# A hybrid decoder layer: weights scaled on ScalarE, slopes folded into the queries, the value tile in quarters

## The reference, cut to what matters

```python
def index_scores(qi, wi, ki, qpos, kpos):
    s = jnp.einsum('bthd,bsd->bths', qi, ki).astype(jnp.float32) * (IDX_DIM ** -0.5)
    s = jnp.einsum('bths,bth->bts', jax.nn.relu(s), wi.astype(jnp.float32))
def sparse_attend(q, k_sel, v_sel, qpos, sel):           # mixer A
    logits = jnp.einsum('bthd,btkhd->bhtk', q, k_sel).astype(jnp.float32) * (HEAD_DIM ** -0.5)
    dist = (qpos[None, :, None] - sel).astype(jnp.float32)
    logits = logits - alibi_slopes()[None, :, None, None] * dist[:, None]
    p = jax.nn.softmax(logits, axis=-1).astype(v_sel.dtype)
    return jnp.einsum('bhtk,btkhd->bthd', p, v_sel)
def forget_attend(q, k, v, Fq, Fk, qpos, kpos):          # mixer B
    logits = jnp.einsum('bthd,bshd->bhts', q, k).astype(jnp.float32) * (HEAD_DIM ** -0.5)
    logits = logits + (Fq.T[:, :, None] - Fk.T[:, None, :])
    p = jax.nn.softmax(logits, axis=-1).astype(v.dtype)
    return jnp.einsum('bhts,bshd->bthd', p, v)
```

## Time and profile before

| | us |
|---|---|
| median of three runs | 1120.89 |
| the profiled execution | 1125.59 |
| its span, first to last instruction | 1123.4 |
| TensorE busy | 1005.9 (90%) |
| VectorE busy | 571.9 (51%) |
| ScalarE busy | 399.5 (36%) |
| GpSimd busy | 170.0 (15%) |
| head pairs 1 to 8 | 125.5 to 418.0 |

### The profile page before, as it was taken

The page is one execution under the profiler, slowest core; times in us unless marked ns, Lnnn a source line. Parts: engine busy times, 40 slices in busy tenths (PEclk is TensorE's granted clock), DMA queues, the critical chain, the costliest instruction groups (busy, mean ns, idle before and its releaser), DMA issues.

```text
span 1123.4 us, 20111 instructions
## 1 busy us (share of the span) xinstructions
PE 1005.9 (90%) x7616; PEld 917.1 (82%) x7616; DVE 571.9 (51%) x1299; ACT 399.5 (36%) x803; POOL 170.0 (15%) x122
## 2 busy tenths in 40 slices
PE   8798878998899889549989999599989999998998
PEld 6596666887788778547389999489989999998998
DVE  3544799776575661554038844564433224443232
ACT  3344444444445442112064544443421113332111
POOL 3003222322342232230003232000000000000000
PEclk9899989998999899778979999799999999999999
DMA  9431521322121224783616665323222333332322
GB/s 351 135 82 33 158 76 48 87 57 57 47 76 48 59 57 120 231 270 121 235 57 206 189 205 176 89 57 94 85 75 87 91 93 94 93 91 71 90 66 76
DMA packets 184106, 124.54 MB, mean 111 GB/s; under 512 B 14419, under 2 KB 168083, under 8 KB 184036
## 3 DMA queue, kind: packets, MB, share of 16 engines
q1 hardware_dynamic: 183906, 123.50, 36.5%
q10 hardware_dynamic: 130, 0.10, 0.0%
HBM read 116.99 MB, written 6.59 MB: 110 GB/s over the span
## 4 chain that ended last, share of the span: by engine, by line
PE 79%; DVE 8%; DMA 4%; ACT 3%; issue 3%; POOL 2%; SPq 1%; ACTq 0%; DVEq 0%; POOLq 0%
PE bank L863 21%; PE bank L864 20%; PE bank L865 20%; DMA qbc<-q_d 3%; PE bank L968 2%; PE bank L945 2%; PE bank L954 2%; PE bank L1116 1%; POOL prod L770 1%; PE bank L782 1%; PE bank L1007 1%; PE bank L804 1%; PE bank L986 1%; DVE w_lo L1725 1%; PE bank L923 1%
## 5 line engine op out<-in xcount | busy, mean ns | idle before, releaser
L863 PE MATMUL bank<-h_hi,w_hi 128*128 128x260 f32 x1360 | 411.0, 302 | 32.9 <-DVE h_lo L1668 17.7
L864 PE MATMUL bank<-h_lo,w_hi 128*128 128x260 f32 x1360 | 400.1, 294 | 0.0
L865 PE MATMUL bank<-h_hi,w_lo 128*128 128x260 f32 x1360 | 399.1, 293 | 0.0
L863 PEld LDWEIGHTS bank<-h_hi,w_hi 128*128 128x128 f32 x1360 | 273.2, 201 | 50.0 <-issue 41.7
L864 PEld LDWEIGHTS bank<-h_lo,w_hi 128*128 128x128 f32 x1360 | 273.3, 201 | 0.2
L865 PEld LDWEIGHTS bank<-h_hi,w_lo 128*128 128x128 f32 x1360 | 272.6, 200 | 0.0
L740 POOL TENSOR_TENSOR w_lo<-raw,w_hi 128x1024 fp32r<-128x1024 f32 x44 | 104.8, 2381 | 420.5 <-ACT w_hi L1311 253.7
L863 PE MATMUL bank<-u_hi,w_hi 128*128 128x260 f32 x512 | 146.5, 286 | 7.7 <-DVE u_lo L2120 7.7
L2105 DVE TENSOR_TENSOR w_lo<-raw,w_hi 128x1024 fp32r<-128x1024 f32 x62 | 76.0, 1226 | 145.7 <-ACT w_hi L1543 145.7
L864 PE MATMUL bank<-u_lo,w_hi 128*128 128x260 f32 x512 | 146.0, 285 | 0.0
L865 PE MATMUL bank<-u_hi,w_lo 128*128 128x260 f32 x512 | 145.9, 285 | 0.0
(11 more groups left out here) (317 smaller groups left out, 1320.3 us busy)
## 6 DMA issues: line engine op xcount, KB each, us to landing
raw<-in_w_in SPq DMA_DIRECT2D x44, 512.0 KB, 3.7
raw<-in_w_ada SPq DMA_DIRECT2D x32, 512.0 KB, 4.0
raw<-in_w_up SPq DMA_DIRECT2D x32, 512.0 KB, 3.9
raw<-in_w_down SPq DMA_DIRECT2D x32, 512.0 KB, 3.9
ada<-in_w_ada SPq DMA_DIRECT2D x4, 2048.0 KB, 12.7
kv<-in_cache_k_b SPq DMA_DIRECT2D x16, 256.0 KB, 3.0
qbc<-q_d SPq DMA_DIRECT2D x16, 256.0 KB, 4.4
kv<-in_cache_k_a SPq DMA_DIRECT2D x16, 256.0 KB, 3.4
```

What stands on the lines that cost most here:

```text
L863: mm(out, hi[:, k, :], x_h, start=first and k == ks[0], stop=False)
L864: mm(out, hi[:, k, :], x_l, start=False, stop=False)
L865: end = mm(out, lo[:, k, :], x_h, start=False, stop=last and k == ks[-1])
```

## The change

Five edits. `probs` on VectorE becomes a reciprocal alone, and the scaling an activation on ScalarE, at the head of its slot. The slope of mixer A isn't multiplied into the distances any more: the queries are divided by it (gq gets five columns), and exp multiplies by it. The value tile's halves are projected in quarters of 12 matmuls, in slots 4, 5, 6 and 7. The low halves of weights are made on VectorE in pair 0 and from pair 4 on, and on GpSimd in pairs 1 to 3. The index scores go through banks 4 to 7 instead of 4 and 5.

```diff
-HALVES_AT = [0, 1, 2, 3, 4, 6]
+HALVES_AT = [0, 1, 2, 3, 5, 7]
+FIRST_HALF_AT = [4, 6]
+        gq = new("gq", [P, 5])
+        def unit_slope(U):
+            m, c = pair_mixer(U // 8)
+            return SLOPES[2 * c + U % 2] if m else 1.0
@@ GpSimd
+            link(pool.memset(gq_scale[:, 0:1], QK_SCALE))
+            for hh in range(2):
+                for c in range(H // 2):
+                    last = pool.memset(gq_scale[64 * hh:64 * hh + 64, 1 + c:2 + c], QK_SCALE / SLOPES[2 * c + hh])
...
             for p, s in ITERATIONS:
-                for i in split_at(p, s):
-                    rest_w(i)
+                if 1 <= p <= 3:
+                    for i in split_at(p, s):
+                        rest_w(i)
@@ TensorE
+            def project(i, half, ks=range(NCH)):
+                if ks[0] == 0:
...
+                end = half_tile(i, half, bank[half + 4 * par(i)][:, 0:HALF], ks, first=ks[0] == 0, last=ks[-1] == NCH - 1)
+                if ks[-1] == NCH - 1:
+                    end.then_inc(proj_done, 1)
             def index_scores(n):
-                if n >= 2:
-                    pe.wait_ge(idx_relu, n)
+                if n >= 4:
+                    pe.wait_ge(idx_relu, n - 2)
...
-                    mm(bank[4 + hh][:, 0:width(qb)], q_idx[rows, h // 2, qb * P:(qb + 1) * P], ki2[rows, 0:width(qb)],
+                    mm(bank[4 + n % 4 + hh][:, 0:width(qb)], q_idx[rows, h // 2, qb * P:(qb + 1) * P], ki2[rows, 0:width(qb)],
@@ TensorE, in the iterations
-                if s in HALVES_AT and (p, s) < (N_PAIRS + 1, 4):
+                if s < 4:
                     project(T_PAIR + 3 * p + HALVES_AT.index(s) // 2, HALVES_AT.index(s) % 2)
+                elif p <= N_PAIRS:
+                    if s in FIRST_HALF_AT:
+                        project(T_PAIR + 3 * p + 2, FIRST_HALF_AT.index(s), range(4))
+                    else:
+                        project(T_PAIR + 3 * p + 2, HALVES_AT.index(s) % 2, range(4, NCH))
@@ ScalarE
-                A(lg[:, U % 3, 0:w], lg[:, U % 3, 0:w], ACT.Exp, bias=stat[:, 8 + U % 8:9 + U % 8],
+                A(lg[:, U % 3, 0:w], lg[:, U % 3, 0:w], ACT.Exp, bias=stat[:, 8 + U % 8:9 + U % 8], scale=unit_slope(U),
...
+            def probs(U):
+                w = width(U % 8 // 2)
+                act.wait_ge(inv_ready, U + 1)
+                A(lg[:, U % 3, 0:w], lg[:, U % 3, 0:w], ACT.Copy, scale=stat[:, 26 + U % 2:27 + U % 2]).then_inc(p_ready, 1)
...
                 before = slot_before(p, s)
+                if 0 <= U - 1 < N_UNITS:
+                    probs(U - 1)
@@ VectorE
-                    if U == 32:
-                        dve.wait_ge(stored, 64)
...
-                    link(dve.tensor_scalar(abias[:, 0:w], src, SLOPES[2 * c + hh], None, ALU.mult))
                     dve.wait_ge(s_done, U + 1)
-                    link(dve.tensor_tensor_reduce(out[:, 0:w], s_bank[:, 0:w], abias[:, 0:w], 1.0, TAKEN, ALU.add, ALU.max, mx))
+                    link(dve.tensor_tensor_reduce(out[:, 0:w], s_bank[:, 0:w], src, 1.0, TAKEN, ALU.add, ALU.max, mx))
...
-            def probs(U):
-                w = width(U % 8 // 2)
+            def inverse_sum(U):
                 dve.wait_ge(e_ready, U + 1)
-                link(dve.reciprocal(stat[:, 25:26], stat[:, 16 + U % 8:17 + U % 8]))
-                dve.tensor_scalar(lg[:, U % 3, 0:w], lg[:, U % 3, 0:w], stat[:, 25:26], None, ALU.mult).then_inc(p_ready, 1)
+                dve.reciprocal(stat[:, 26 + U % 2:27 + U % 2], stat[:, 16 + U % 8:17 + U % 8]).then_inc(inv_ready, 1)
@@ VectorE, in the iterations
                 if p == 0:
+                    for i in split_at(p, s):
+                        rest_w(i)
...
+                if p >= 4:                     # after logits(U)
+                    for i in split_at(p, s):
+                        dve.wait_ge(lo_ready, i)
+                        rest_w(i)
```

More of the change, by code:

```diff
@@ L173, in layer @@
         g_col = new("g_col", [P, 2])
-        gq = new("gq", [P, 2])
+        gq = new("gq", [P, 5])
         gk_row = new("gk_row", [P, 2, HD])
@@ L219, in layer @@
         p_t = new("p_t", [P, 2, 2, QB, P])
+        gq_scale = sb("gq_scale", [P, 5], F32, place["at"])[0]
         place["at"] += 8192
@@ L373, in layer @@
         e_ready = sem("e_ready")
+        inv_ready = sem("inv_ready")
         p_ready = sem("p_ready")
@@ L403, in layer @@
         s_consts = sem("s_consts")
+        gq_consts = sem("gq_consts")
         kip_landed = sem("kip_landed")
@@ L728, in _ @@
             pool.memset(s8[:, 11, :], 0.0).then_inc(s_consts, 1)
+            link(pool.memset(gq_scale[:, 0:1], QK_SCALE))
+            for hh in range(2):
+                for c in range(H // 2):
+                    last = pool.memset(gq_scale[64 * hh:64 * hh + 64, 1 + c:2 + c], QK_SCALE / SLOPES[2 * c + hh])
+                if hh == 0:
+                    link(last)
+            last.then_inc(gq_consts, 1)
             def power(n):
@@ L892, in first_tiles @@
                                 last.then_inc(proj_done, 1)
[L894 to L903, removed]
+            def project(i, half, ks=range(NCH)):
+                if ks[0] == 0:
+                    if half == 0:
+                        pe.wait_ge(hi_ready, i + 1)
+                        pe.wait_ge(lo_ready, i + 1)
+                    if i >= 1:
+                        before = i - 1 if par(i - 1) == par(i) else i - 2
+                        pe.wait_ge(act_evac, act_evac_value(before, half))
+                end = half_tile(i, half, bank[half + 4 * par(i)][:, 0:HALF], ks, first=ks[0] == 0, last=ks[-1] == NCH - 1)
+                if ks[-1] == NCH - 1:
+                    end.then_inc(proj_done, 1)
             def ada_product(g, half):
@@ L1374, in store_back @@
             def store_back(p, kd):
-                m = pair_mixer(p)[0]
+                m, c = pair_mixer(p)
+                col = 1 + c if m else 0
                 act.wait_ge(back_done, 2 * p + kd + 1)
@@ L1379, in store_back @@
                         act.wait_ge(s_done, 8 * (p - 1))
-                    A(q_fm[:, p % 2, :], bank[3][:, :], ACT.Copy, scale=gq[:, m:m + 1]).then_inc(back_read, 1)
+                    A(q_fm[:, p % 2, :], bank[3][:, :], ACT.Copy, scale=gq[:, col:col + 1]).then_inc(back_read, 1)
                 else:
@@ L1401, in relu_scores @@
                     act.wait_ge(smt_done, 1)
-                A(rbuf[:, n % 2, 0:w], bank[4 + n % 2][:, 0:w], ACT.Relu).then_inc(idx_relu, 1)
+                A(rbuf[:, n % 2, 0:w], bank[4 + n % 4][:, 0:w], ACT.Relu).then_inc(idx_relu, 1)
             def ada_rows(g):
@@ L1745, in _ @@
             dve.wait_ge(small_landed, 16 * N_SMALL)
-            dve.tensor_scalar(gq[:, :], g_col[:, :], QK_SCALE, None, ALU.mult)
+            dve.wait_ge(gq_consts, 1)
+            dve.tensor_tensor(gq[:, 0:1], gq_scale[:, 0:1], g_col[:, 0:1], ALU.mult)
+            dve.tensor_tensor(gq[:, 1:5], gq_scale[:, 1:5], g_col[:, 1:2].to_broadcast([P, 4]), ALU.mult)
             def index_sum(n):
@@ L1807, in logits @@
                                                   ALU.add, ALU.max, mx))
-                dve.tensor_scalar(nm, mx, -1.0, None, ALU.mult).then_inc(lg_ready, 1)
-            def probs(U):
-                w = width(U % 8 // 2)
+                dve.tensor_scalar(nm, mx, -unit_slope(U), None, ALU.mult).then_inc(lg_ready, 1)
+            def inverse_sum(U):
                 dve.wait_ge(e_ready, U + 1)
-                link(dve.reciprocal(stat[:, 25:26], stat[:, 16 + U % 8:17 + U % 8]))
-                dve.tensor_scalar(lg[:, U % 3, 0:w], lg[:, U % 3, 0:w], stat[:, 25:26], None, ALU.mult).then_inc(p_ready, 1)
+                dve.reciprocal(stat[:, 26 + U % 2:27 + U % 2], stat[:, 16 + U % 8:17 + U % 8]).then_inc(inv_ready, 1)
             def mean_squares(p, kd):
@@ L1949, in _ @@
                 if 0 <= U - 1 < N_UNITS:
-                    probs(U - 1)
+                    inverse_sum(U - 1)
                 if 0 <= U < N_UNITS:
                     logits(U)
+                if p >= 4:
+                    for i in split_at(p, s):
+                        dve.wait_ge(lo_ready, i)
+                        rest_w(i)
                 if p < N_PAIRS:
```

## The result

The changed kernel took 1112.13 us (median of 11 runs, 1105.13 to 1115.97) against 1121.73 for the kernel before (median of 11, 1118.17 to 1125.46): a ratio of 0.991, 95% interval 0.9885 to 0.9935. The direction was right. The size was not: 9.6 us against a forecast of 32, and 1112 lies outside the range of 1068 to 1107. The profiled execution lasted 1115.97 us, its span 1114.0 against 1123.4.

A forecast was written before the change was run, and what follows sets the result against it. The attention stage was taken as a four-engine loop whose latency shows twice a pair, where the clock can fall too. Pair gains plus 1.2 at the end sum to 32 us: 1125.6 to 1093.6 profiled, median 1089; range 1068 to 1107.

The forecast's parts named there:

- the sum of pairs 1 to 3: Pairs 0 and 1 together -10 us, pair 2 -3.1, pair 3 -2.6, though the scale waits behind VectorE's reciprocal.
- Pair 0: Four index-score banks remove 9.5 us of waits; late forget rows leave 2.3 there; with pair 1, -10 us (bounds 5 and 14).
- Pair 3: VectorE and the keys' chain set the pace; 35.2 us taken for pairs 2 and 3 alike, so -2.6 here.
- Pairs 4 to 7: Quarters shorten slots 4 to 7: 34.3, then 33.4 us each, including 0.7 for a slow stretch behind the keys' wait.
- The scale's price: 64 more ScalarE activations at 0.35 to 0.65 us, 4.0 us a pair, duration hidden.
- The slopes: Folding the slopes removes a VectorE operation that ran while waiting for scores: gain 0 (bounds 0 and 2 us).
- The last low half: End of the attention stage, before the store of queries: 1.23 us on VectorE replaces 2.43 on GpSimd, -1.2.
- B: Rival: ScalarE's queue blocks, half a us lost in each of slots 4 to 7, 16 us in all: 1105; chance 0.14.
- D: Rival: slower, two more engine crossings cost 1.0 us a unit, 64 us uncovered: 1153; chance 0.06.
- A: Rival: keys' chain doesn't bind, clock stays at 2.4 GHz; -50 us, 1071; chance 0.15.
- C: Rival: the port; VectorE's low halves meet GpSimd's power, ten times 1.6 us from pair 4 to 8: 1105; chance 0.04.
- E: Rival: all hidden anyway, pairs stay and pair 0's gain is lost; within 5 us, 1119; chance 0.06.

The follow-up runs named there:

- recip_early: Changed kernel, but in pairs 1 to 4 VectorE takes the reciprocal in the middle of the selection round; 1098.41 us, ratio 0.9806.
- only_scale: Kernel before with one edit: the scaling as an activation at the head of ScalarE's slot; 1134.89 us, ratio 1.0111.
- only_scale_ordered: Kernel before with scaling on ScalarE, but page copies ahead of the scale and the reciprocal in the middle of the selection round; 1119.65 us, ratio 0.9978.
- low_on_gpsimd: Changed kernel, but the low halves stay on GpSimd from pair 4 on too; 1107.04 us, ratio 0.9878.
- fbc_first: Changed kernel, but SP loads the forget rows of pair 1 before the 48 page transfers; 1103.53 us, ratio 0.9846.
- all_orders: Changed kernel: page copies before scale, reciprocal mid selection round, forget rows before pages, low half behind mean and last o_lo from pair 4; 1090.48 us.
- orders_low_five: all_orders with slot 4's low half moved behind the keys' multiplications, to the end of slot 5; 1084.40 us, ratio 0.966.
- scale_late: Changed kernel, but VectorE scales in pairs 1 to 3 (units 0 to 23) as before; 1113.39 us, ratio 0.9925.
- orders_scale_late: orders_low_five, but VectorE scales in pairs 1 to 3, its reciprocal after the selection round; 1100.30 us, ratio 0.9816.
- only_quarters: Kernel before with one edit: the value tile projected in quarters; 1110.56 us, ratio 0.9887.

## Why the prediction was wrong, step by step

*The step that failed* is the sum of pairs 1 to 3. The prediction wrote that the scale waits "behind VectorE's reciprocal, which stands behind the selection round", and priced it: "the squares of slot 4 and GpSimd's w_lo are later by about 1.2 us". It named the right wait, and followed it to two of the instructions behind it. It left out the page copies and z_s, which stand there too and hold banks that TensorE wants: 3.0, 4.3 and 3.0 us in single waits, where the prediction had 1.2 us in slot 4. It also took the result to be "needed two slots later": that counts from the scores; from the scale it is one slot, and it didn't bind (no wait at L973 is over 1.2 us). Forecast for pairs 0 and 1 together -10, measured -1.5; pair 2 -3.1, measured +4.8; pair 3 -2.6, measured +2.0. That is 21.0 of the 22.4 us by which the profiled execution missed the sum. The bounds did not hold it either: "0 and the 6.5 us" for pairs 2 and 3 had no loss in them, though a new wait at the head of a queue can cost, and that was the second error. The cause is shown by recip_early (-13.7 us with the work unchanged, the waits for ki_pt 0.5 for 7.4) and by only_scale against only_scale_ordered (15 us). The parts done alone don't add up to the whole: quarters -12.5, banks -4.4, scale +11.9, and +5.1 for the low halves from pair 4 on (the changed kernel less low_on_gpsimd) give 0.1; measured -9.6. Which parts help each other is not shown, and pair 0's low halves and the slopes had no run of their own.

*Pair 0* went as argued as far as fbc. Rows of the tile after, 100 to 130 us, beside the earlier trace rows:

```profile
L591 SPq DMA_DIRECT2D fbc<-negf_d x4: 433/594/1672, 115.7 to 124.1; - x4
L1977 DVE TENSOR_TENSOR fdiag<-fbc,cmask x2: 691/692/693, 121.6 to 122.4; 128x512 f32<-128x512 f32 x2
...
  DMA fbc<-negf_d: 5.5, 1
```

VectorE waited 5.5 us and started at 121.6, where 121.7 was forecast. The slot 2 wait of TensorE came as well (3.0 us), but through ScalarE: z_s behind the scale behind VectorE. That VectorE would then need only 31 us for the pair did not come true: it took 39.1, to 160.7. fbc_first shows what the late forget rows cost: 8.6 us.

*Pair 3* was given pair 2's 35.2 us without a look at its own row: TensorE was busy for 35.5 us there, 2.4 more than in pair 2; among other things a step of the sample group stands in its slot 6 (32 matmuls of 8 columns, L1029 before, 3.74 us). The 35.5 us are no floor, for part of them ran at 1.2 GHz. all_orders shows pair 3 at the full clock:

```profile
184.76:222.26 37.50, 33.18 (x274) 28.82 (x273) 26.08 (x83) 20.72 (x52) 10.92 (x5) 1.00 0.22 62
```

So 35.2 would have left 2.0 us for waiting. TensorE waited 4.3 us there, 2.9 for p_t and 1.4 for the keys, with ki_pt and z_s out of the way. In orders_low_five, alike in this pair, the same two waits and a clock of 0.92 gave 40.5; that difference is clock.

*Pairs 4 to 7* were right: 34.3, 33.4, 33.4 and 33.4 forecast, 34.7, 32.8, 33.7 and 33.6 measured. Pair 8 took 31.5, not 30.0. In sum the four agree (134.5 and 134.7 us), but the waits in them are not all where they were forecast. Pair 5 shows which parts were right. Timeline after, slots 4 to 6, beside the earlier trace rows (slot 4's turn is at 293.99):

```profile
296.23 0.56 DVE L1829 CUSTOM_DVE_ANT_0 lg<-bank,sel 128x384 f32<-128x384 f32 x1 [2.69 <-PE bank L964]
296.91 1.23 DVE L1757 TENSOR_TENSOR w_lo<-raw,w_hi 128x1024 fp32r<-128x1024 f32 x1
298.05 0.68 DVE L1847 TENSOR_REDUCE ms<-sq 128x8 f32<-128x512 f32 x1
298.14 0.41 PE L973 MATMUL bank<-ident,lg 128*128 128x128 f32 x2 [0.41 <-ACT p_t L1394]
298.84 0.68 DVE L1866 TENSOR_TENSOR o_lo<-bank,o_hi 128x512 fp32r<-128x512 f32 x1
299.01 1.64 POOL L750 TENSOR_TENSOR rs<-ms,neghalf 128x8 f32<-128x8 f32 x1 [6.27 <-DVE ms L1848]
299.67 0.44 PE L987 MATMUL bank<-p_t,v_tok 128*64 128x128 f32 x4 [1.13 <-DVE o_lo L1866]
301.41 0.69 DVE L1862 TENSOR_TENSOR tok<-tok,gk_row 128x512 f32<-128x512 f32 x1
302.15 0.44 PE L1016 MATMUL bank<-ident,tok 128*128 128x128 f32 x2 [0.40 <-DVE tok L1862]
```

The keys are ready at +8.1 (302.10 less 293.99), where +8.3 was forecast, and TensorE comes to them at +8.2 (forecast +8.3). But it does not wait 1.9 us there. The wait is in three: 0.41 for p_t, 1.13 before the values for o_lo, 0.40 at the keys. The o_lo, behind the low half and the mean on VectorE, was not foreseen; it takes its time out of the keys' wait, so the sum held. The 0.7 us added for a slow stretch did not come in pair 5 (clock 1.00): the sum without it, 32.7, is what was measured.

*The scale's price.* L1387 takes 402, 508, 616 and 720 ns by width, 0.05 to 0.07 us above the 0.35 to 0.65 taken, and as dear as exp. (The Trainium skill, page "ScalarE: Activation LUTs", section "What ACT_TABLE_LOAD costs", gives 280 ns + 0.833 ns a column where one operand is a pointer by partition; an estimate from it is 387 to 706 ns. The trace agrees within 4 per cent.) It was hidden.

*The slopes* cost and gave nothing that these traces show: VectorE still waits 2.69 us for the scores before L1829 (above). No kernel changed them alone, so this is argued. *The last low half* came as forecast, in the timeline of the end of the stage beside the earlier trace rows:

```profile
423.18 1.23 DVE L1757 TENSOR_TENSOR w_lo<-raw,w_hi 128x1024 fp32r<-128x1024 f32 x1 [6.58 <-ACT w_hi L1335]
424.32 0.68 DVE L1866 TENSOR_TENSOR o_lo<-bank,o_hi 128x512 fp32r<-128x512 f32 x1
...
424.90 0.43 SPq L582 DMA_DIRECT2D q_d<-ts_a  x1
```

1.23 us stands there instead of 2.43, and behind that store the stage is as long as before (9.5 us earlier at the store, 9.4 at the end).

*The rivals.* B, "ScalarE's queue blocks", had the mechanism, and with 1105 was nearest. It had the place wrong: half a us in each slot 4 to 7 of all pairs, where in fact pairs 4 to 7 lost nothing, and slot 2 of pair 1 and the ends of pairs 1 and 2 lost 3.0 to 4.3 us each. D's loss a unit did not come: no wait at L973 is over 1.2 us. A, with no wait for the keys, is refuted in pair 5 (0.40 and 1.13 us). C: the low halves on VectorE take 1.22 us on the mean, not 2. E: the pairs from 4 on did get shorter.

**What stays open.** Why pair 3 is so long, at so low a clock, in three kernels: scale_late, orders_scale_late and only_quarters, with 48.2, 46.8 and 44.6 us. These are the three that have quarters in pair 3 while VectorE scales there. Every other kernel has 37.5 to 41.0. In these three TensorE's waits in pair 3 are 3.8 to 3.9 us for p_t and 1.9 for the keys, about 1.5 more together than in all_orders (2.9 and 1.4); its busy time is 42.5, 41.1 and 38.9 us, against 33.2 there at the full clock. So most of the length is clock. Why the clock stays low for so long after waits that are little longer was not tested, and all of this is from single profiles.

## What to carry to other kernels

An operation moved to another engine brings its wait with it, and in a queue served in order everything behind it inherits that wait: list all that stands behind it and who waits for each, also the small copies that have nothing to do with the change. Put an operation whose result is wanted late behind the ones that others wait for, and what feeds another engine's head of queue (here 0.16 us of reciprocal) as early as its input allows. Where cover is cut in one place (the four banks, the shorter slots), ask which load or producer now sets the start, since 11 us of head start were worth 4.4 while the forget rows came late.
